# Fetching the experts' tokens with matmuls on rounded float32 pairs, two expert pairs at a time

## What is computed

```python
top_v, top_i = lax.top_k(e_sel, TOP_K_INNER)          # 2 of 32 experts for each token
for gi in range(N_EXPERT_GROUPS):
    hg = jnp.einsum('td,edf->tef', t, w_gate[gi])
    hu = jnp.einsum('td,edf->tef', t, w_up[gi])
    act = (jax.nn.silu(hg) * hu * combine[:, gi, :, None].astype(t.dtype)).astype(t.dtype)
    out = out + jnp.einsum('tef,efd->td', act, w_down[gi]).astype(f32)
...
h = _layernorm(DN_ALPHA * h1 + moe + ple, ln2_w[i], ln2_b[i])
```

## Time and profile before

| | us |
|---|---|
| median of 3 runs | 947.07 (946.57 to 948.12) |
| span of the profiled execution | 947.1 |
| PLE matmuls end | 587.6 |
| first `gate_up` starts | 600.3 |
| last `down` ends | 903.0 |
| from there to the end of the span | 44.1 |

### The profile page before, as it was taken

How to read it: one execution, slowest core, us unless ns; L and a number is a source line. 1 busy time by engine, 2 the same in 40 slices (tenths; PEclk the granted TensorE clock), 3 DMA queues, 4 the chain that set the end, 5 groups by cost and what they waited for, 6 DMA issues and landing times.

```text
span 947.1 us, 11294 instructions
## 1 busy us (share of the span) xinstructions
PE 840.8 (89%) x4489; PEld 584.5 (62%) x4489; DVE 426.3 (45%) x780; ACT 176.5 (19%) x331; POOL 151.3 (16%) x74
## 2 busy tenths in 40 slices
PE   0599997799999999999999998999999999999910
PEld 0488787788888885444448887756565556555600
DVE  6999534455688883112365763112111211121128
ACT  4222223453232220000002010111111111111112
POOL 6734741110123111000004000000000000000032
PEclk9999998899999999999999999999999999999965
DMA  9524231111121226230007462359999999999452
GB/s 307 193 90 89 82 97 45 45 45 46 46 78 56 57 78 233 78 126 31 21 0 253 148 206 106 97 201 359 357 357 371 361 360 356 367 363 358 153 183 106
DMA packets 119296, 163.42 MB, mean 173 GB/s; under 512 B 14412, under 2 KB 102614, under 8 KB 118742
## 3 DMA queue, kind: packets, MB, share of 16 engines
q1 hardware_dynamic: 113184, 139.68, 45.1%
q0 software_dynamic: 3072, 12.63, 3.7%
q10 hardware_dynamic: 2998, 10.53, 2.8%
HBM read 148.15 MB, written 14.68 MB: 172 GB/s over the span
## 4 chain that ended last, share of the span: by engine, by line
PE 83%; DVE 8%; DMA 4%; ACT 2%; issue 2%; POOL 0%; ACTq 0%; SPq 0%; DVEq 0%; POOLq 0%
PE psum L732 23%; PE psum L1010 14%; PE psum L1022 12%; PE psum L1037 6%; PE psum L941 6%; PE psum L931 6%; PE psum L980 4%; PE psum L922 3%; DMA ring<-in_w_in_dram 2%; DVE arena L1378 2%; ACT arena L1090 2%; DVE arena L1377 2%; PE psum L871 2%; PE psum L891 1%; PE psum L982 1%
## 5 line engine op out<-in xcount | busy, mean ns | idle before, releaser
L732 PE MATMUL psum<-ring_r 128*128 128x512 f32 (+1 forms) x768 | 213.2, 363 | 2.6 <-DVE arena L1549 1.3
L732 PEld LDWEIGHTS psum<-ring_r 128*128 128x128 f32 x768 | 139.4, 194 | 26.1 <-issue 2.4
L1010 PEld LDWEIGHTS psum<-arena 128*128 128x128 f32 x1088 | 125.5, 194 | 28.4 <-issue 25.1
L1010 PE MATMUL psum<-arena 128*128 128x128 f32 x1088 | 131.6, 280 | 2.9 <-DVE arena L1702 2.9
L667 POOL TENSOR_TENSOR ring_r<-ring,ring_r 128x2048 fp32r<-128x2048 f32 x20 | 93.4, 4670 | 205.3 <-ACT ring_r L1090 205.3
L1090 ACT COPY arena<-psum 128x512 f32<-128x512 f32 (+3 forms) x104 | 58.5, 582 | 351.8 <-PE psum L948 139.8
L1022 PE MATMUL psum<-ring,arena 128*64 128x512 f32 x512 | 113.4, 595 | 7.9 <-ACT arena L1090 7.9
L732 PE MATMUL psum<-arena_r,ring_r 128*128 128x512 f32 x256 | 100.4, 392 | 0.0
L1797 DVE SCALAR_TENSOR_TENSOR arena<-arena,psum 128x256 f32<-128x256 f32 x16 | 6.7, 421 | 186.5 <-ACT arena L1268 186.5
L1022 PEld LDWEIGHTS psum<-ring,arena 128*64 128x64 f32 x512 | 37.1, 137 | 73.9 <-issue 65.5
L695 POOL DMA_INDIRECT ring<-y_rows,rowsU x8 | 8.1, 1017 | 389.4 <-ACT arena L1090 387.2
(11 more groups left out here) (240 smaller groups left out, 875.8 us busy)
## 6 DMA issues: line engine op xcount, KB each, us to landing
ring<-in_w_exp_gate_dram SPq DMA_DIRECT2D x32, 1024.0 KB, 12.1
ring<-in_w_exp_up_dram SPq DMA_DIRECT2D x32, 1024.0 KB, 12.5
ring<-in_w_exp_down_dram SPq DMA_DIRECT2D x32, 1024.0 KB, 9.1
ring<-in_w_in_dram SPq DMA_DIRECT2D x18, 1024.0 KB, 5.3
y_rows<-arena ACTq DMA_DIRECT2D x16, 512.0 KB, 7.6
y_rows<-arena POOLq DMA_DIRECT2D x4, 1024.0 KB, 7.3
ring<-in_w_out_ssd_dram SPq DMA_DIRECT2D x4, 1024.0 KB, 7.4
ring<-in_w_out_dram SPq DMA_DIRECT2D x4, 1024.0 KB, 11.0
```

Source lines behind the costliest of these rows:

```text
L732: t = mm(o, a, b, start=(first and j == 0), stop=(last and j == 2))
L1010: t = mm(o[:, k, :], h[:, i, c:c + P], onehot[:, buf, i, :], start=(i == 0), stop=(i == NT - 1))
```

## The change

- `h1` is split into two tiles of rounded float32: `h_hi` (a ScalarE copy that rounds, one for each 128 tokens) and `h_lo` (what is left, a VectorE subtraction, `h1_rest`). They take the places of `hT` and of `h`. The copies stand between the last four of ScalarE's PLE steps, the subtractions at the end of VectorE's PLE loop.
- The fetch multiplies both tiles by a one-hot matrix of 256 columns, which holds two pairs, so a fetch number q serves pairs 2q and 2q+1. It has four parts of 16 matmuls, 128x128 by 256 columns in rounded float32, one instruction each. Step p does two of the parts of the fetch for the next two pairs, both ahead of `down(p-1)`.
- The steps 14 and 15 fetch nothing. The first fetch serves pairs 0 and 1; its four parts have PSUM banks of the plan (`("xf", n)`).
- VectorE writes one-hot matrices of 256 columns, every second step. The second of them is written behind the PLE loop and no longer ahead of it.
- `xgT` has two buffers of 256 columns. `gate_up` reads its half of one.
- The hardware loops over the steps are written out on every engine.
- The column numbers that are compared (`iota_c`) are written by GpSimd later, with a semaphore of their own.

```diff
-            def fetch(half, buf, part):
-
-                if not (isinstance(half, int) and half < 2):
-                    pe.wait_ge(s_xgT_sb, half - 1)
-                o = psum[:, 2 + 5 * part, :].rearrange("p (k t) -> p k t", k=4)
-                for k in range(4):
-                    c = (4 * part + k) * P
-                    for i in range(NT):
-                        t = mm(o[:, k, :], h[:, i, c:c + P], onehot[:, buf, i, :], start=(i == 0), stop=(i == NT - 1))
+            def gathered(o, q, k, width):
+
+                for i in range(NT):
+                    mm(o, h_hi[:, k, i, :], onehot[q % 2][:, i, 0:width], start=(i == 0), stop=False)
+                    t = mm(o, h_lo[:, i, k, :], onehot[q % 2][:, i, 0:width], start=False, stop=(i == NT - 1))
+                return t
+
+            def fetch(q, part):
+
+                n = 4 * q + part
+                pe.wait_ge(s_xgT_sb, n - 1)
+                o = psum[:, 2 + 5 * (part % 2), :].rearrange("p (k t) -> p k t", k=2)
+                for k in range(2):
+                    t = gathered(o[:, k, :], q, 2 * part + k, 2 * P)
                 t.then_inc(s_xT_mm, 1)
...
-                gate_up(e4 * 2 + u // 2, u, u % 2, p * 2 + 2)
-                pe.wait_ge(s_onehot_ready, p + 2)
-                fetch(p * 2 + 2, 1 - u % 2, 0)
-                if not start:
-                    down(p - 1, e4 * 2 + (u - 1) // 2, (u - 1) % 4)
-                fetch(p * 2 + 3, 1 - u % 2, 1)
-                act_t(p, u)
...
             pe.wait_ge(s_onehot_ready, 1)
-            for part in range(2):
-                fetch(part, 0, part)
...
+            pe.wait_ge(s_h1_lo, NT)
+            for part in range(4):
+                o = opened(("xf", part)).rearrange("p (k t) -> p k t", k=2)
+                for k in range(2):
+                    t = gathered(o[:, k, :], 0, 2 * part + k, 2 * P)
+                t.then_inc(s_xT_mm, 1)
+            for s, v in plan_last:
+                pe.wait_ge(s, v)
+            for p in range(PAIRS):
+                q = p // 2
+                gate_up(q, p % 2, q % 2, P * (p % 2), 4 * q + 4)
+                if q < PAIRS // 2 - 1:
+                    pe.wait_ge(s_onehot_ready, q + 2)
+                    fetch(q + 1, 2 * (p % 2))
+                    fetch(q + 1, 2 * (p % 2) + 1)
+                if p:
+                    down(p - 1, (p - 1) // 2, (p - 1) % 2)
+                act_t(p, p % 2)
...
-            for i in range(4 * NT):
-                act.wait_ge(s_pg_read, i + 1)
-                A(pgt[:, i % 4, :], pgt[:, i % 4, :], ACT.Tanh, scale=0.5).then_inc(s_pg_tanh, 1)
...
+            for n in range(4 * NT):
+                if n >= 3 * NT:
+                    i = n - 3 * NT
+                    act.wait_ge(s_pe_pl, n + 1)
+                    copy(h_hi[:, :, i, :], h[:, i, :].rearrange("p (k n) -> p k n", k=KD)).then_inc(s_h1_hi, 1)
+                act.wait_ge(s_pg_read, n + 1)
+                A(pgt[:, n % 4, :], pgt[:, n % 4, :], ACT.Tanh, scale=0.5).then_inc(s_pg_tanh, 1)
...
+            def h1_rest(i):
+                dve.wait_ge(s_h1_hi, i + 1)
+                v.tensor_tensor(h_lo[:, i], h[:, i, :].rearrange("p (k n) -> p k n", k=KD), h_hi[:, :, i, :].bitcast(F32),
+                                ALU.subtract).then_inc(s_h1_lo, 1)
```

More of the change, by code:

```diff
@@ L200, in psum_plan @@
             unit("rk", 1, ("rk_read", 1))
+    for n in range(4):
+        unit(("xf", n), 1, ("xgT_sb", n + 1))
     place, holder, at = {}, [[] for _ in range(8)], 0
@@ L341, in block_kernel @@
         ctlf = at(region(EXTRA + 2), EXTRA + 2)
[L342 to L343 removed]
+        second = shaped(R_A + 5120, "p (i r) -> p i r", i=NT, r=2 * P)
+        iota_c = at(R_DT, 2 * P)
         rowf = shaped(region(2 * NT), "p (i c) -> p i c", i=NT, c=2)
@@ L589, in _ @@
             gate_slice(3)
[L590 to L594, removed]
+            for p in range(1, PAIRS):
+                experts(p)
             sp.wait_ge(s_ctl_ready, 1)
@@ L1024, in gate_up, with down @@
                 t.then_inc(s_gu_mm, 1)
-            def down(p, former, u):
+            def down(p, former, parity):
                 for half in range(2):
-                    expert_slot_in(pe, former, u % 2, half, 2)
+                    expert_slot_in(pe, former, parity, half, 2)
                 pe.wait_ge(s_aT_sb, p + 1)
@@ L1074, in _ @@
                 with pe.If(pairs > j):
-                    pe.wait_ge(s_onehot_ready, j + PAIRS + 3)
-                    for part in range(2):
-                        fetch(j * 2 + 2 * PAIRS + 2 + part, 0, part)
-                    gate_up(j + PAIRS // 2, 0, 0, j * 2 + 2 * PAIRS + 4)
+                    pe.wait_ge(s_onehot_ready, j + PAIRS // 2 + 1)
+                    for part in range(4):
+                        pe.wait_ge(s_xgT_sb, j * 4 + 2 * PAIRS + part - 1)
+                        o = psum[:, 2 + 5 * (part % 2), :].rearrange("p (k t) -> p k t", k=2)
+                        for k in range(2):
+                            t = gathered(o[:, k, 0:P], 0, 2 * part + k, P)
+                        t.then_inc(s_xT_mm, 1)
+                    gate_up(j + PAIRS // 2, 0, 0, 0, j * 4 + 2 * PAIRS + 4)
                     act_t(j + PAIRS, 0)
@@ L1282, in out_copy @@
                 act.dma_start(y_dram[bass.ds(p * 2 * CAP, 2 * CAP)], eout[:, u % 2, :]).then_inc(y_st[u % 2], 16)
-            def step(e4, u):
-                p = e4 * 4 + u
-                hidden_tanh(p, u)
-                rows_copy(p * 2 + 2, 1 - u % 2, 0)
-                if not (isinstance(e4, int) and u == 0):
-                    out_copy(p - 1, e4 * 32 + 16 * ((u - 1) // 2), (u - 1) % 4)
-                rows_copy(p * 2 + 3, 1 - u % 2, 1)
-                act_copy(p, u)
-            act.wait_ge(s_pe_mix, 2 * NT)
-            rows_copy(0, 0, 0)
-            rows_copy(1, 0, 1)
-            for u in range(4):
-                step(0, u)
-            with act.Fori(1, PAIRS // 4) as e4:
-                for u in range(4):
-                    step(e4, u)
-            out_copy(PAIRS - 1, 16 * (PAIRS // 2 - 1), 3)
+            act.wait_ge(s_pe_mix, 2 * NT)
+            for part in range(4):
+                rows_copy(part, 0, part, bank(("xf", part)), 2 * P)
+            for p in range(PAIRS):
+                q = p // 2
+                hidden_tanh(p, p % 2)
+                if q < PAIRS // 2 - 1:
+                    for part in (2 * (p % 2), 2 * (p % 2) + 1):
+                        rows_copy(4 * q + 4 + part, (q + 1) % 2, part, psum[:, 2 + 5 * (part % 2), :], 2 * P)
+                if p:
+                    out_copy(p - 1, 16 * ((p - 1) // 2), (p - 1) % 2)
+                act_copy(p, p % 2)
+            out_copy(PAIRS - 1, 16 * (PAIRS // 2 - 1), 1)
             pairs = act.value_load(ctl[0:1, EXTRA + 1:EXTRA + 2], min_val=0, max_val=MORE_PAIRS)
@@ L1305, in _ @@
                     p = j + PAIRS
-                    for part in range(2):
-                        rows_copy(j * 2 + 2 * PAIRS + 2 + part, 0, part)
+                    for part in range(4):
+                        rows_copy(j * 4 + 2 * PAIRS + part, 0, part, psum[:, 2 + 5 * (part % 2), :], P)
                     hidden_tanh(p, 0)
@@ L1806, in out_half @@
                 v.tensor_copy(eout[:, u % 2, 512:1024], psum[:, 5, :]).then_inc(s_y_dve, 1)
-            def step(e4, u):
-                p = e4 * 4 + u
-                hidden(p, u)
-                tokens_rows(p + 2, u % 2, p * 2 + 2, p + 2)
-                if not (isinstance(e4, int) and u == 0):
-                    out_half(p - 1, e4 * 32 + 16 * ((u - 1) // 2), (u - 1) % 4)
-            for u in range(4):
-                step(0, u)
-            with dve.Fori(1, PAIRS // 4) as e4:
-                for u in range(4):
-                    step(e4, u)
-            out_half(PAIRS - 1, 16 * (PAIRS // 2 - 1), 3)
-            dve.wait_ge(s_rowf_moved, PAIRS + 2)
-            v.tensor_scalar(rowf, rowf, 4.0 * CAP, None, ALU.add).then_inc(s_rowf_moved, 1)
+            for p in range(PAIRS):
+                q = p // 2
+                hidden(p, p % 2)
+                if p % 2 == 0 and q + 2 < PAIRS // 2:
+                    tokens_rows(q + 2, q % 2, 4 * q + 4, q + 2, 4 * CAP)
+                if p:
+                    out_half(p - 1, 16 * ((p - 1) // 2), (p - 1) % 2)
+            out_half(PAIRS - 1, 16 * (PAIRS // 2 - 1), 1)
             pairs = dve.value_load(ctl[0:1, EXTRA + 1:EXTRA + 2], min_val=0, max_val=MORE_PAIRS)
```

105 lines of the change are left out of this document (53 added, 52 removed).

## The result

The changed kernel takes 961.18 us (median of four runs, 958.88 to 962.56) against 947.60 for the kernel before on the same chip. The ratio is 1.0139, with a 95% interval of 1.0126 to 1.0151. The forecast was 937.6, with a range up to 948.5. The profiled execution has a span of 959.0 us; the device time is 1.8 us longer than the span, in this and in the later runs.

A forecast was written before the change was run, and what follows sets the result against it. TensorE's step (18.89 us) and the loads (18.80 us a pair) were taken as balanced, the loads limiting next. Terms: -2.2 us at the start, 0 in between, -7.3 at the end; 947.1 - 9.5 = 937.6 us, range 930.5 to 948.5.

The forecast's parts named there:

- What bounds the kernel: Pair loop: TensorE's step of 18.89 us and the loads' 18.80 us a pair in balance; faster TensorE then waits for weights.
- The fetch: TensorE, each step: matmuls of 0.120 us, so 3.84 us a step in place of 7.54; saving in steps 2 to 13 becomes idle.
- The end of the kernel: Last landing to end of last `down`: 17.5 us in place of 24.8, with 2.0 for the clock; term -7.3 us.
- The run of loads: From pair 2's first down load to the last landing: 248.3 us unchanged, down loads issued 4.2 us ahead of the next landing.
- Rival 2: Pair loop: half clock makes `down` late and starves the load queue; steps of 20.3 us, 956 us; chance 0.05 in full.
- milder form: Same starved queue in the pair loop, with a step of 19.3 to 20 us; chance 0.07.
- Rival 1: Pair loop: loads go faster when asked for earlier, 4.2 us of notice in place of 2.6; about 932 us; chance 0.12.
- The test named for being wrong: Wrong if `gate_up` starts under 18.4 or over 19.1 us apart, fetch starts after 594, or mid-loop DMA share under 1.

The follow-up runs named there:

- e6_gates_first: Changed kernel with SyncE issuing the gate and up loads of pair p+1 ahead of the down loads of pair p, from p = 2 on: 922.83 us, ratio 0.9735.
- e3_down_first: Changed kernel with down(p-1) directly behind gate_up(p) and the whole fetch behind it: 933.57 us, ratio 0.9838.

## Why the prediction was wrong

*What bounds the kernel* was read rightly. TensorE's step and that of the loads are almost equal, and the loads are the limit behind it: no kernel here got under 18.4 us a pair in the mean.

*The fetch* costs what was said. The first one of the changed kernel and its wait:

```profile
587.50 2.36 DVE L1793 TENSOR_TENSOR arena_r<-arena,arena_r 128x1024 fp32r<-128x1024 f32 x2
...
589.96 0.36 PE L1007 MATMUL psum<-arena_r 128*128 128x256 f32 x1 [3.87 <-issue]
...
600.12 7.09 PE psum L1030 x32
...
911.09 3.65 PE L1045 MATMUL psum<-ring,arena 128*64 128x512 f32 x16 [1.41 <-ACT arena L1101]
```

The two subtractions take 1.2 us each. The idle time is 3.9 us (4.1 said), and from the end of the PLE matmuls to `gate_up(0)` it is 14.0 us (14.25 said). `down(0)` ends 40.0 us after them, 40.1 said. The end of the kernel took 18.5 us from the last landing, 17.5 said: the last `gate_up` lost 2.3 us to the clock, near the forecast (2.0), it started 0.25 us behind the landing, and the last `down` waited 1.4 us for ScalarE's copy of the transposed activation (the last row above), where 0.88 were said.

*The run of loads* is the step that failed: "I take 248.3 unchanged". It was 270.1. The question asked there was the right one, whether the queue stays fed, and the answer, "4.2 us ahead of the next landing", was worked out for a steady step at full clock. Three things were wrong in it.

First, the loop does not begin in the steady state. The prediction's own numbers put the end of `down(0)` at 627.7; carried on, the end of `down(1)` comes near 642.7 and the landing of pair 3, 22.6 us after 627.7, at 650.3. That is an idle time of over 7 us ahead of `gate_up(3)`. It was 8.7 us, and I did not write it down. Instead the rival was judged by an idle time of 3.9 us.

Second, the clock was charged where nothing hides it, in the first fetch and at the end, and 1.7 us in a step "by the rows", but not in the 4.2 us of notice on which the 248.3 rested. With 7.7 to 8.8 us of idle time `gate_up` took 9.4 to 9.9 us, 2.3 to 2.8 more, and a `down` ended 17.2 to 17.7 us after a landing. The notice was then from 0.4 to -0.6 us.

Third, the next landing was taken to come 18.8 us after the last. With down loads that went out 8 us early it came after 17.0 to 18.1, and that took the rest of the notice.

*Rival 2* said this: a starved queue, steps of 20.3 us, 956. Measured are 20.5 and 961. Its mechanism and price were right and its chance of 0.12, milder form included, was the mistake. Its counterargument, that one drop leaves TensorE too little idle time for the next, assumed even steps. They alternate: one step has no idle time and the next has all of it. The rule of the Trainium skill that was weighed there (TensorE: Matmul & The Clock Gate, "HAM oscillation — how this bites in real kernels") describes such a loop, in which each wait for a load brings the engine back to half clock. The trace agrees, in every second step. The rows had nothing against it, since they held no idle time as long as these within the loop.

*Rival 1*, loads that go faster when asked for earlier, is true on its own: 18.4 to 18.5 us a pair in e6_gates_first and e3_down_first, where 18.35 was given as the lower bound. It needed the notice that the changed kernel didn't give. The figure near 358 GB/s that the Trainium skill gives (DMA: Bandwidth & Descriptors, "Where 436 GB/s comes from") is not a limit here: 374 GB/s was held over 207 us.

*A small slip* was to take the span of the profiled execution for a device time: that is 1.8 us longer in every run whose two numbers are known. It changes neither sign nor size.

*The test named for being wrong* was met: `gate_up` starts further apart than 19.1 us, and a DMA share under 1 in mid-loop (0.98).

## What to carry to other kernels

When an engine gets faster and a load queue is next, count the notice that each load gets before the queue runs dry, from the first step on and at half clock, not in the steady state alone. If it is short (in the kernel before 2.6 to 4.0 us kept the queue fed, in the changed one 0.4 us and less did not), let loads with an early release pass those with a late one, or move the releasing work forward: one change of SyncE's order turned a loss of 1.4% into a gain of 2.7%. Idle time of TensorE is not free when the work behind it releases the next load.

## What the hardware did that I had not expected

- The granted clock fell 3.3 us into an idle time of 8.0 us (682.83 to 686.17, then 0.50) and stayed there for 5.6 us of the matmuls that followed. Before the loop an idle time of 2.9 us was followed by 3.41 us at 0.50.
- Useless matmuls in the idle time made the kernel faster, by 18 us.
- A queue whose last load had landed 0.6 us before the next issue took until 23.1 us after the next issue for a landing that a fed queue brings every 18.4 us. With the short step before it, a double step takes 41.0 us instead of 36.8. The 4.2 us lost are about the pause in the rates, from 666 to 670 us, and not the 0.6 us between landing and issue: the bytes stop before the landing shows and begin again at least 0.5 us behind the issue.
